# All projections in one stretch as rounded products beside the threshold search, gates in DRAM, one attention loop

## What is computed

```python
def token_mixers(h, cos, sin, w_in, b_forget, w_out_a, w_out_b, w_out):
    ...
    qa, ka, va, qi, ki, wi, qb, kb, vb, fb, ga, gb = _split_cols(h @ w_in)
    ...
        score = jnp.einsum('bqh,bqhs->bqs', wi_blk.astype(jnp.float32), jax.nn.relu(rel))
        ...
        _, sel = lax.top_k(score, topk)
    ...
        logit = logit + jnp.swapaxes(cq_blk, 1, 2)[..., None] - cum_t[:, :, None, :]
    ...
    ya = oa.reshape(B, S, N_HEADS_A * HEAD_DIM) @ w_out_a
    yb = ob.reshape(B, S, N_HEADS_B * HEAD_DIM) @ w_out_b
    merged = jax.nn.sigmoid(ga) * ya + jax.nn.sigmoid(gb) * yb
    return merged @ w_out

def hier_moe(h, w_group, b_group, w_router, b_router, w_e_gate, w_e_up, w_e_down):
    ...
        hid = jax.nn.silu(xb @ w_e_gate[e]) * (xb @ w_e_up[e])
        return hid @ w_e_down[e]
```

## Time and profile before

| | us |
|---|---|
| median of 3 runs | 1739.41 (1737.37 to 1742.87) |
| profiled execution | 1740.7, span 1738.9 |
| busy TensorE / VectorE / ScalarE | 1609.8 / 1028.3 / 550.6 |
| DMA moved | 315.72 MB |
| granted TensorE clock, mean | 0.969 |

### The profile page before, as it was taken

One profiled execution on the slowest core, in us unless ns is written; L12 is line 12 of the kernel. 1 busy time (PEld: TensorE's weight loads), 2 busy tenths in 40 slices (PEclk: granted clock), 3 DMA queues, 4 the chain that ended last, 5 costly groups with the idle time before them and its releaser, 6 DMA issues.

```text
span 1738.9 us, 23746 instructions
## 1 busy us (share of the span) xinstructions
PE 1609.8 (93%) x8184; PEld 905.2 (52%) x8185; DVE 1028.3 (59%) x2041; ACT 550.6 (32%) x1116; POOL 198.9 (11%) x372
## 2 busy tenths in 40 slices
PE   6999999999999888999999996699999999999992
PEld 3563456564654555788888885233333333333330
DVE  6766787887877777688888755423333333333323
ACT  4214554453543677232233321111111111111113
POOL 0110000000000000000000000122222222222221
PEclk9999999999999999999999997799999999999996
DMA  9552201010000030234532725899989747999995
GB/s 363 201 194 74 74 25 37 25 49 1 1 1 0 13 74 1 73 75 106 157 74 72 281 85 200 338 390 381 320 326 395 285 142 250 406 403 340 410 402 217
DMA packets 128306, 315.72 MB, mean 182 GB/s; under 512 B 14237, under 2 KB 75717, under 8 KB 103649
## 3 DMA queue, kind: packets, MB, share of 16 engines
q1 hardware_dynamic: 116482, 297.86, 45.9%
q0 software_dynamic: 11744, 16.82, 4.3%
HBM read 299.64 MB, written 25.99 MB: 187 GB/s over the span
## 4 chain that ended last, share of the span: by engine, by line
PE 85%; DVE 5%; DMA 4%; ACT 3%; issue 2%; SPq 1%; POOL 0%; POOLq 0%; ACTq 0%; DVEq 0%
PE ps L1408 20%; PE ps L1426 9%; PE ps L1310 7%; PE ps L1311 7%; PE ps L1312 7%; PE ps L1193 5%; PE ps L1218 4%; PE ps L1243 4%; PE ps L1199 3%; PE ps L1114 3%; PE ps L1255 3%; PE ps L1229 2%; DVE arena L1717 2%; PE ps L1152 2%; PE ps L1165 2%
## 5 line engine op out<-in xcount | busy, mean ns | idle before, releaser
L1408 PE MATMUL ps<-arena 128*64 128x512 f32 x1632 | 377.0, 605 | 14.0 <-issue 10.8
L2028 DVE COPY arena<-ps 128x256 f32<-128x256 f32 x51 | 21.7, 425 | 403.9 <-ACT arena L1030 403.9
L1408 PEld LDWEIGHTS ps<-arena 128*64 128x64 f32 x1632 | 114.7, 139 | 229.5 <-issue 218.9
L1310 PE MATMUL ps<-rounded 128*128 128x512 f32 x512 | 200.5, 392 | 2.4 <-DVEq L1831 2.4
L1312 PE MATMUL ps<-rounded 128*128 128x512 f32 x512 | 199.9, 391 | 0.0
L1311 PE MATMUL ps<-rounded 128*128 128x512 f32 x512 | 199.9, 390 | 0.0
L1426 PE MATMUL ps<-arena 128*64 128x512 f32 x816 | 183.8, 592 | 0.5 <-ACT arena L1034 0.5
L1652 DVE TENSOR_SCALAR_CACHE_REDUCE arena<-arena,small 128x384 bf16<-128x384 f32 (+2 forms) x192 | 171.1, 940 | 0.0
L1717 DVE CUSTOM_DVE_ANT_0 arena<-ps,arena 128x896 f32<-128x896 f32 (+7 forms) x128 | 91.8, 754 | 65.8 <-PE ps L1218 62.3
L762 POOL DMA_INDIRECT sum_rows<-arena,ones x51 | 81.4, 1597 | 406.1 <-DVE arena L2050 396.8
L1426 PEld LDWEIGHTS ps<-arena 128*64 128x64 f32 x816 | 58.7, 137 | 116.4 <-issue 116.4
(11 more groups left out here) (303 smaller groups left out, 2200.8 us busy)
## 6 DMA issues: line engine op xcount, KB each, us to landing
arena<-in_w_e_up_dram SPq DMA_DIRECT2D x64, 1024.0 KB
arena<-in_w_e_gate_dram SPq DMA_DIRECT2D x64, 1024.0 KB
arena<-in_w_e_down_dram SPq DMA_DIRECT2D x32, 2048.0 KB
arena<-in_w_mod_dram SPq DMA_DIRECT2D x12, 2048.0 KB, 9.4
arena<-in_w_in_dram SPq DMA_DIRECT2D x48, 512.0 KB, 4.9
arena<-in_x_dram SPq DMA_DIRECT2D x16, 512.0 KB, 7.0
arena<-cum_rows SPq DMA_DIRECT2D x8, 512.0 KB, 5.4
arena<-in_w_out_a_dram SPq DMA_DIRECT2D x16, 256.0 KB, 5.6
```

The source lines that it names most:

```text
L1310: pe.matmul(out, w_h, a_h, start=first, stop=False)
L1408: m = pe.matmul(ps[o * TB:(o + 1) * TB, 2, 0:2 * FQ].rearrange("p (j n) -> p j n", j=2), xT[:, k % NX, k // NX * TB:(k // NX + 1) * TB], w ...
```

## The change

All products with `w_in` after the index projection become three rounded products, in one stretch on TensorE before any attention unit. The 16 "slots" of two 128-column tiles are: 8 for the gates (slot 0 takes the place of the first Q/K pieces among the index scores), 2 for Q of A, 4 for Q and K of B, 2 for V of B. h is split into `h_hi`, `h_lo` once, kept by token tile. ScalarE takes the sigmoid of the gates from PSUM and SyncE stores them to `gate_rows` in DRAM. VectorE runs the whole threshold search beside this stretch. Then all 64 units run in one loop: VectorE does maxima, scaling and output copies for both branches, and TensorE does three transposes of unit n, the scores of n+3, the other transposes, then all values of n-1. Transposed probabilities have 8 buffers instead of 4. Modulation rows are stored and loaded back broadcast. The merging rounds have only `ya` and `yb`; gates are loaded back. In the experts ScalarE takes the sigmoid and VectorE two products in place of a copy, an addition, a reciprocal and two products.

```diff
+            def by_tokens(s, j, kt, bank, half):
+                cols = slice(kt * P, (kt + 1) * P)
+                return three_products(ps[:, bank, :].rearrange("p (t n) -> p t n", t=4), slot_hi(s, j)[:, cols], slot_lo(s, j)[:, cols],
+                                      h_hi4[half][:, :, kt, :], h_lo4[half][:, :, kt, :], kt == 0, kt == KT - 1)
+
+            def by_columns(s, t, out):
+                w_h, w_l = (fr(slot_at(s) + a, 2 * U, [2, KT, P]) for a in (2, 0))
+                for kt in range(KT):
+                    m = three_products(out.rearrange("p (j n) -> p j n", j=2), h_hi[t][:, kt, :], h_lo[t][:, kt, :],
+                                       w_h[:, :, kt, :], w_l[:, :, kt, :], kt == 0, kt == KT - 1)
+                return m
...
-            for n in range(-LEAD, FIRST_OF_THREE):
-                scores(n + LEAD)
...
+            for m in GATE_SLOTS:
+                for j in range(2):
+                    gate(m, j)
...
+            for q in range(2 * TT):
+                qa_tile(q)
+            for p in range(PAIRS):
+                for j in range(2):
+                    raw_tile(p, j)
+                    qa_turn(2 * p + j)
+            for v in range(5):
+                v_tiles(v)
+
+            for n in range(-LEAD, N_U + 1):
+                groups = len(key_groups(n)) if 0 <= n < N_U else 0
+                for f in range(min(groups, 3)):
                     turn_p(n, f)
...
                 if n + LEAD < N_U:
                     scores(n + LEAD)
...
+                for f in range(3, groups):
                     turn_p(n, f)
+                if n < 0:
+                    v_tiles(8 + n)
+                if n >= 1:
+                    for f in range(len(key_groups(n - 1))):
+                        values(n - 1, f)
...
+            for u in range(N_G):
+                half, z, bank = u // KT, u % 2, 2 * (u % 4)
+                pe.wait_ge(mg_done, max(2, u - 1))
+                pe.wait_ge(wlo_ok, u + 1)
...
+            act.wait_ge(xt_act, TT + 6)
+            act.wait_ge(xt_dve, TT + 10)
             for t in range(TT + 1):
                 if t < TT:
+                    high_h(t)
                     project_out(t)
...
+            def low_h(t):
+                dve.wait_ge(h_rounded, t + 1)
+                dve.wait_ge(ip_ps, t + 1)
+                dve.tensor_tensor(h_lo[t], hT[t], h_hi[t].bitcast(F32), ALU.subtract).then_inc(h_rest, 1)
...
+                low_h(t)
                 mod_sums(4 + t)
 
-            dve.wait_ge(f_ln, 1)
+            for j in range(2):
+                low_slot(0, j)
+            dve.wait_ge(f_exp, 2)
...
-                link(dve.tensor_scalar(e, e, 1.0, None, ALU.add))
-                link(dve.reciprocal(e, e))
+                e, bank = gates[u % 4], 2 * (u % 4)
+                dve.wait_ge(gate_in[u % 4], 32 * (u // 4) + 32)
...
+            low_m(0)
+            low_m(1)
...
-                taken = chain.up(dve.tensor_copy(gu, ps[:, 2, 0:FQ]))
-                plus = chain.up(dve.tensor_scalar(sg[z], sg[z], 1.0, None, ALU.add))
...
+                link(dve.tensor_tensor(gu, sg[z], ps[:, 2, 0:FQ], ALU.mult))
```

More of the change, by code:

```diff
@@ L183, in at, with fr @@
             a = arena[:, int(u * U):int(u * U) + n]
+            if shape is not None:
+                names = " ".join(f"a{k}" for k in range(len(shape)))
+                a = a.rearrange(f"p ({names}) -> p {names}", **{f"a{k}": s for k, s in enumerate(shape)})
+            return a
+        def fr(u, n, shape=None):
+            if n <= U:
+                a = rounded[int(u)][:, int(u % 1 * U):int(u % 1 * U) + n]
+            else:
+                a = pairs[(u - 1) // 2][:] if n == 2 * U else quads[u // 4][:]
             if shape is not None:
@@ L295, in build @@
         m_hi = [[half_tile(u).rearrange("p (k n) -> p k n", n=P) for u in us] for us in m_at]
-        m_lo = [rounded[16 + kt][:] for kt in range(KT)]
+        m_lo = [fr(16 + kt, U) for kt in range(KT)]
         x1 = [at(u, U) for u in (34, 35, 41, 28, 30, 31, 32, 33)]
@@ L552, in _ @@
[L552 to L564 removed]
+            for j in range(2):
+                sp.wait_ge(gate_ok, 2 * j + 2)
+                gate_store(0, j)
@@ new lines, in gate, with mod_row @@
+            def gate(m, j):
+                k = 2 * (m - 1) + j
+                pe.wait_ge(slot_rest, 2 * m + j + 1)
+                if k >= 3:
+                    pe.wait_ge(gate_ok, 4 + k - 2)
+                for kt in range(KT):
+                    for half in range(2):
+                        x = by_tokens(m, j, kt, 2 * (k % 3) + half, half)
+                x.then_inc(gate_ps, 1)
+            def mod_row(n):
+                if n == 0:
+                    pe.wait_ge(acc_ok, 10)
+                    pe.wait_ge(gate_ok, 4)
+                if n >= 2:
+                    pe.wait_ge(mrow_ok, n + 1)
+                pe.matmul(ps[0:1, 6 + n % 2, :], ones[:, 0:1], acc[2 + n // 2][:, n % 2 * 512:n % 2 * 512 + 512], start=True, stop=True).then_inc(mrow_ps, 1)
@@ L1559, in _ @@
                 if kt % 3:
-                    dve.tensor_scalar(hT[:, kt, :], hT[:, kt, :], a1[:, kt:kt + 1], sh1[:, kt:kt + 1], ALU.mult, ALU.add).then_inc(xt_dve, 1)
+                    for half in range(2):
+                        dve.tensor_scalar(hT4[half][:, :, kt, :], hT4[half][:, :, kt, :], a1[:, kt:kt + 1], sh1[:, kt:kt + 1], ALU.mult, ALU.add).then_inc(xt_dve, 1)
             dve.wait_ge(freq_ok, HALF)
@@ new lines, in _ @@
+            room = {s: 19.0 - {KT: 0, KT + 1: 8, KT + 2: 4, KT + 3: 4}.get(s, 0) for s in range(1, SLOTS)}
+            parts, k, at_cost, at_room = {s: [] for s in room}, 0, 0, 0
+            for s in range(1, SLOTS):
+                at_room += room[s]
+                while k < len(steps) and (at_cost + steps[k][0] / 2) * sum(room.values()) <= at_room * sum(c for c, _ in steps):
+                    at_cost += steps[k][0]
+                    parts[s].append(steps[k][1])
+                    k += 1
@@ new lines, in _ @@
+            assert k == len(steps)
+            for s in range(1, SLOTS):
+                early = len(parts[s]) // 2
+                for step in parts[s][:early]:
+                    step()
+                if s + 1 < SLOTS:
+                    for j in range(2):
+                        low_slot(s + 1, j)
+                if s == KT + 1:
+                    for q in range(TT):
+                        rope_a(q)
+                if KT + 2 <= s < KT + 4:
+                    for q in range(TT + 4 * (s - KT - 2), TT + 4 * (s - KT - 2) + 4):
+                        rope_a(q)
+                for step in parts[s][early:]:
+                    step()
```

823 lines of the change are left out of this document (381 added, 442 removed).

## The result

The changed kernel takes 1816.79 us (median of 4 runs, 1810.58 to 1819.36), the kernel before 1739.88 us (4 runs beside it, 1737.37 to 1742.87): ratio 1.0436, 95% interval 1.0403 to 1.047. It is 77 us slower; the forecast was 1708 us and 32 us faster. The profiled execution took 1810.58 us, with a span of 1808.8.

What follows compares the result with a forecast made beforehand. TensorE was taken as the bound, except in branch A's attention units. 207.5 - 2 + 601.5 (projections, attention) + 114 (merging) + 5.4 + 780.6 (rest) = 1707 us of span, forecast 1707.5 us; 8 in 10 range 1676 to 1738.

Steps and rivals of the forecast that it cites:

- I carry everything after 958.3 us over: 780.6 us: Output projection with router, experts and end: matrix products kept, shorter silu and sigmoid table hidden behind TensorE, 780.6 us unchanged.
- if the experts' stage changes length: Experts: one of three signs that the prediction is wrong; it expected this stage unchanged at 607 us.
- score stage ends: Index score stage, 134.5 to 207.5 before: cheaper rounded products against later weights, net -2 us, between -6 and +5.
- projections, V tiles, first scores: Projection stretch: TensorE sets the pace for 326.1 us with the threshold search covered, then 25 us to the first transposition.
- attention loop and its end: All attention units: the wait on VectorE's output copy goes, 248 us (bounds 236 and 270), plus 2.4 us end.
- merging, and the wait of the first output tile: Merging rounds: weight loads no longer fully covered, 114 us (87 to 125); then the first output tile waits.
- The 5.4 us of the prediction: First output tile: waits for the last merge and one split of merged rows, and starts at the lower clock, +5.4 us.
- Rival 4: Projections: 256 wide rounded products cost as much as 512 wide ones, +82 us, 1790; chance 0.07.
- Rival 1: Attention loop keeps its waits, units stay at 33.8 us per eight, +22 us, 1730; chance 0.13.
- rival 3: Loads land faster or the loop meets its bound: merging near 92 us, attention near 236, total 1673 to 1680; chance 0.12.
- rival 2: Merging rounds run at the lower clock, 18.1 us a pair, 138 us in all, total 1731; chance 0.11.
- the sum of 1707 us: Whole span: all forecast stages added, 1707 us against 1738.9 before, -32 us; forecast case's chance 0.52.

Runs made afterwards that it cites:

- Experiments 1 and 2: Idle TensorE instructions put ahead of the experts: 76 in the changed kernel, 1686.45 us; 180 in the kernel before, 1886.35 us.
- experiment 4: Kernel before with only the change's new silu (ScalarE sigmoid, two VectorE products) and hid_ok wait in the experts: 1738.93 us, ratio 0.9997.

## Why the prediction was wrong

**The step that failed** is one sentence: "I carry everything after 958.3 us over: 780.6 us", with the cover named for it, that the experts are full on TensorE. I had read TensorE's rows as if their supply of instructions cost nothing and only semaphores could delay them. The change makes TensorE's program ahead of the experts 2228 instructions longer by the count, and I priced each by its products, not by where it leaves the code behind it. Experiments 1 and 2 show that place alone, in either kernel, makes and unmakes the loss. Of the conditions under which the prediction called itself wrong, the last one came true: "if the experts' stage changes length". No rival held it, so the range ended at 1738.

The rows of before had a trace of it, and I passed over them: "issue" gaps ahead of the first products at the first three branches of the experts' stage, and then none until the last expert, which stands outside the loop. Order of time, TensorE, kernel before:

```profile
1117.35 3.65 PE L1408 MATMUL ps<-arena 128*64 128x512 f32 x16 [1.79 <-issue]
...
1130.80 3.65 PE L1408 MATMUL ps<-arena 128*64 128x512 f32 x16 [1.87 <-issue]
...
1146.18 6.23 PE L1408 MATMUL ps<-arena 128*64 128x512 f32 x16 [3.78 <-issue]
```

A stall that comes in the first round only is code that is kept from then on; a reader can ask by how little.

**The other steps**, each by its own number (the run with 76 idle instructions has the same products in the same stages, so it stands for the rest where the stalls of the experts would hide it):

| step | forecast | measured |
|---|---|---|
| score stage ends | 205.5 | 206.0 |
| projections, V tiles, first scores | 326.1 + 25 | 350.7 |
| attention loop and its end | 248 + 2.4 | 238.5 |
| merging, and the wait of the first output tile | 114 + 3.7 | 109.1 |
| rest of the span | 1.7 + 780.6 | 904.5 (778.4 with 76) |

The measured column adds up to 1808.8 us. The 5.4 us of the prediction are split here: 3.7 us of waiting, which the trace has ahead of the mark at 904.3 (3.88 us), and 1.7 for the lower clock. The prediction speaks of three last rows of the stage table; the earlier trace rows has two of them, and the end of the span (26.9 us) is in its 780.6 all the same.

The projections were right to the microsecond (206.0 to the first scores at 532.6), and by the right reasons: TensorE without idle time (323.06 of 323.06 us), and the 256 wide rounded products at the price taken by the narrow f32 rows. Five starts, four distances of 0.12 us:

```profile
395.74 0.28 PE L1194 MATMUL ps<-rounded_pair,rounded_quad 128*128 128x256 f32 x1
395.86 0.28 PE L1192 MATMUL ps<-rounded_pair,rounded_quad 128*128 128x256 f32 x1
395.98 0.28 PE L1193 MATMUL ps<-rounded_pair,rounded_quad 128*128 128x256 f32 x1
396.10 0.28 PE L1194 MATMUL ps<-rounded_pair,rounded_quad 128*128 128x256 f32 x1
396.22 0.28 PE L1192 MATMUL ps<-rounded_pair,rounded_quad 128*128 128x256 f32 x1
```

Rival 4 (1790) is out. The Trainium skill's figure of 109 ns for this width (TensorE: Matmul & The Clock Gate, section "Back-to-back issue gap") is the gap that it gives for an isolated product, without the load of weights that stands ahead of each one here; it is 9% below the 120 ns of this trace, as it was 5% below at 512 columns.

**The attention loop** was over-sized by 11.9 us. VectorE's first 1024 wide maxima of two successive head pairs:

```profile
578.00 1.22 DVE L1771 CUSTOM_DVE_ANT_0 arena<-ps,arena 128x1024 f32<-128x1024 f32 x1 [2.43 <-PE ps L1315]
...
608.31 1.23 DVE L1771 CUSTOM_DVE_ANT_0 arena<-ps,arena 128x1024 f32<-128x1024 f32 x1 [2.43 <-PE ps L1315]
```

30.3 us a pair among the B heads, where I took 32, with 2 us added for VectorE: it waits 2.43 us for TensorE there, so it is not the late one. Rival 1 (the units keep their 33.8 us) is out; the attention half of rival 3 came true.

**Merging** was over-sized by 8.6 us. Columns as above, a round's weights, their rounding, the subtraction, and the first product of the next pair:

```profile
815.00 0.38 SPq L591 DMA_DIRECT2D arena<-in_w_out_a_dram  x1
815.43 0.51 SPq L591 DMA_DIRECT2D arena<-in_w_out_b_dram  x1
...
818.82 1.06 ACT L953 ACTIVATE rounded<-arena 128x1024 fp32r<-128x1024 f32 x1 [5.09 <-DMA arena<-in_w_out_b_dram]
...
819.91 1.23 DVE L1866 TENSOR_TENSOR rounded<-arena,rounded 128x1024 fp32r<-128x1024 f32 x1 [2.82 <-ACT rounded L953]
...
821.24 0.47 PE L1192 MATMUL ps<-rounded 128*128 128x512 f32 x1 [0.83 <-issue]
```

The chain is the one forecast, load to rounding to subtraction to product, but the load is ready 3.8 us after its first issue where I took 5.3. A pair lasts 12.0 us (809.25 to 821.24), not 14.1, and its gap of 0.8 us leaves the granted clock at 1.00. The 2 MB for the next matrix do what was forecast (+4 us): one gap of 4.60 us. Behind it, as behind the gap of 1.72 us at the start of the stage, the products begin at the lower clock:

```profile
868.09 0.77 PE L1192 MATMUL ps<-rounded 128*128 128x512 f32 x1 [4.60 <-issue]
```

So rival 2, every pair at the lower clock, is out: the lower clock came at two of the gaps and not at those of 0.8 to 1.3 us, and I had charged it at every second gap. The Trainium skill (TensorE: Matmul & The Clock Gate, section "HAM oscillation — how this bites in real kernels") describes bursts of products that each start at the lower clock after a DMA wait of 3 to 5 us; the gap of 4.60 us agrees, and the one of 1.72 us shows the lower clock behind a shorter one. The trace lists the gap at 821.24 under "issue" although the subtraction ends 0.1 us before the product: a reader can't take the word for a fetch without looking at who else ended there.

Had the loop lain as before, the sum of 1707 us would have met a span of 1684.4: 22.6 us too high. Of it 10.5 us arose before the merging (the attention loop), 8 in the merging, 3 in the output projection and dispatch, 4 in the experts (602.8), and the end took 3 us more. Whether the new silu brought the 4 us is not shown: experiment 4 found no difference in time.

## What to carry to other kernels

A stage that the change leaves alone can still be moved in the store of code. Where an engine runs a long loop with hardware branches, count its instructions with every branch that is never taken, and keep it well under seven pieces of 256; after any change upstream compare the packets of the instruction queue inside the loop, which should be zero after the first round. Where a kernel's time jumps by several per cent and the idle time in front of a branch target is named "issue", look at the code's place before looking for a cause in the change itself: move the loop back, by count, to the place in a piece where it ran well, or shorten it. A shift taken at random proves little: of seven tried here, only two were fast.

## What the runs showed of the hardware

- TensorE's loop of 1773 instructions by the count ran without fetches only at 2 of 8 starts tried in the changed kernel, and one of 1412 at both starts tried. 1821, 48 of them never reached, fetched again in every round.
- When it does not fit, it is fetched again as a whole and not only what hangs over: 8.9 pieces of 16 KB a round, where the loop is 6.9 pieces long by the count and can touch 8. That would fit a store of eight pieces, filled in order, one of which goes to the piece ahead; the Trainium skill (Runtime: NRT & Kernel Launch, section "Instruction fetch mechanics") gives TensorE 2048 instructions, eight pieces, refilled in order. No run here shows the piece ahead by itself, so that reading stays a reading.
- A stall at a branch lasted 0.7 to 11.8 us in the changed kernel and up to 14.7 us in the runs that moved it; with weight traffic at about a third (97 GB/s for 279) it was 6.47 us at most. 80 further packets of 16 KB, 0.6% of the bytes that the experts' stage moves, cost 122 us.
- A semaphore increment on TensorE's queue took 0.139 us in a row of 180 (25.07 us); 96, 128 and 224 of them filled gaps of 12.02, 16.91 and 31.82 us, 0.125 to 0.142 us each.
